# A first pair of projections by eight half products, its operand sums beside it, in a float32 decoder layer

## The chip, the core and the metric

The kernel runs on one core of one Trainium2 chip. The metric is the device time of one execution in microseconds (us). The engines are TensorE (PE; its weight loads are the rows PEld), VectorE (DVE), ScalarE (ACT), GpSimd (POOL) and SyncE (SP), which issues most DMAs. Each runs its own list of instructions in order, and they meet at semaphores: an instruction that waits holds back everything behind it on its engine.

## The reference, cut to what matters

One decoder layer on 1024 tokens of width 1024, all in float32: an input projection feeds a dilated window attention of 12 heads (three groups of four) and a gated DeltaNet of 8 heads; both are gated and merged, and a SwiGLU follows.

```
u = rmsnorm(h, norm_mix[layer])
proj = u @ w_in[layer]
qa, ka, va, qd, kd, vd, z, beta_raw, a_raw, gate_raw = jnp.split(proj, split_at, axis=-1)
...
beta = jax.nn.sigmoid(beta_raw)
g = -jnp.exp(a_log[layer]) * jax.nn.softplus(a_raw + dt_bias[layer])
```

The change concerns the first blocks of `u @ w_in` and how `beta` and `g` are made beside them.

## The kernel before, in words

Activations are held transposed (feature on the partition, 1024 tokens along the row). A float32 matrix product is made of three passes (PASSES): each operand is split into a rounded high part (ACT copies it, L985 for weights) and a low part (POOL or DVE subtracts, L946, L446), and high x high, high x low, low x high are added in a PSUM bank. One matmul has a 128x128 weight block and 512 tokens.

The attention stage makes 24 pairs of 128-column blocks of `w_in`, numbered q = 0 to 23. For unit n = q // 2 (one head; slot s, group g), the even pair gives its queries and keys, the odd pair its values and a block of the gates. A pair by the plain method takes eight half products of 12 matmuls (two blocks, two halves of the tokens, two halves of the 1024 features). The kernel uses Strassen's scheme in Winograd's form and takes seven: PRODUCTS lists them in the order m = 0 to 6 by their weight operand, a, c, s2, s1, s3, s4, d. Weight halves a, c come from `raw_first`, b, d from `raw_second`; s1 = b + d, s2 = s1 - a, s3 = a - b, s4 = c - s2 are made by POOL. The activation operands t1 to t4 are sums of quarters of u (`own_sum_t`), made once by DVE (L488), cast by ACT (operand_cast, L441) and subtracted by DVE (operand_low, L446). They are used by all 24 pairs, as are x11, x21, x22, parts of u itself. t2 is then written over the one quarter of u that is not needed (a copy is kept in DRAM).

The order of the work is written out by hand. Each product has four steps j, so a unit has 56 (j = 0 to 55). At a product's last step ACT takes products 0, 2, 3 and 6 out of PSUM (take_act, L1066), DVE adds 1, 4 and 5 (L1088). Two banks are used in turn, so product m = 2 can start only when product 0 has been taken, m = 4 only when 2 has been taken, and so on (the waits at L1011). Behind these steps ACT casts the next pair's weight operands as HIGH_STEP says, POOL makes that pair's sums and low parts (attention_pool), and SP loads the weights of the pair after it into the same two buffers when the low parts that read them are there (load_first, load_second). Between the matmuls of unit n the softmax steps of unit n - 1 run (att_pe, att_act, at the steps AT: 15 steps for two of the groups, 9 for the third), and at slots 1 to 3 also the mixing of the three groups of the slot before (MIX, with small DMAs that ACT issues at L867 to L873).

Ahead of this stands the set-up: rows of x are scaled (DVE, L457), transposed (PE, L513), weighted (DVE, L472) and split (ACT L417, POOL L356). `beta_decay` (L500) makes the 16 columns for beta and decay in 48 matmuls, 24 of them between the last transposes. The rows of beta and decay are worked out in 40x1024 tiles during unit 0 (decay_act, decay_vec): beta is 1/(1 + exp(-x)), with a reciprocal on DVE (L607).

Of the kernel before, what the change touches and what calls it, by code (L numbers as in the profile page):

```python
# [65 lines left out]
def build(nc, x, norm_mix, w_in, conv_w, a_log, dt_bias, dn_norm, w_proj_attn, w_proj_delta,  # L66
          w_out, norm_ffn, w_gate, w_up, w_down, norm_final, out):
    ctx = ExitStack()
    with ctx:
# [364 lines left out]
        OPERAND = {"t1": 1, "t2": 2, "t3": 3, "t4": 4}  # L434

        def operand_cast(act, o):

# [4 lines left out]

        def operand_low(dve, o):
# [3 lines left out]
                                    ALU.subtract).then_inc(qp["low"], 1)  # L447

        def setup_vec(dve):
# [29 lines left out]
            def part(k_half, t_half):  # L479
                return u32[:, 4 * t_half:4 * t_half + 4, 4 * k_half:4 * k_half + 4, :]  # L480

            def by_chunk(o):
                return own_sum[o][:, :, :].rearrange("p f (c t) -> p c f t", t=P)

            for o, first, second in (("t1", part(0, 1), part(0, 0)), ("t2", part(1, 1), by_chunk("t1")),
                                     ("t3", part(1, 1), part(0, 1)), ("t4", part(1, 0), by_chunk("t2"))):
# [5 lines left out]
            operand_low(dve, "t2")  # L492

        def setup_pe(pe):
# [12 lines left out]
            for c in range(KT):  # L507
# [8 lines left out]
                if c >= KT // 2:  # L516

                    if c == KT // 2:
                        pe.wait_ge(ba_split, 1)
                        pe.wait_ge(x_low, KT)  # L520
                    for k in (2 * c - KT, 2 * c - KT + 1):
                        beta_decay(0, k)
            pe.wait_ge(x_low, 2 * KT)
            for k in range(KT):
                beta_decay(1, k)
# [2028 lines left out]
```

## Time and profile before

| | us |
|---|---|
| median of 3 runs (2327.79 to 2329.65) | 2329.26 |
| profiled execution, its own time | 2330.01 |
| its span in the trace | 2328.3 |
| PE busy | 2205.2 (95% of the span) |
| DVE busy | 1079.8 (46%) |
| ACT busy | 937.3 (40%) |
| POOL busy | 694.2 (30%) |

In 40 slices of 58 us PE is at nine tenths or more in all but the first, one at about 1610 us, one near it and the last; in the first slice it is at five tenths. The granted TensorE clock has a mean of 0.98 of full speed over the span.

A row of the timeline has the start in us, the duration in us, engine, line, operation, tile written <- tiles read, sizes, a count where several are put together, and in brackets how long the engine was idle before it and what ended that. The duration of a matmul in such a row overlaps the next one; from start to start they are 0.227 us apart at full clock, 0.427 at half.

### The profile page before, as it was taken

The numbers are of one execution on the slowest core, as the hardware profiler recorded it, in microseconds if no ns is written. First come the engines' busy times: TensorE is split into PE (matmuls) and PEld (weight loads), VectorE is DVE, ScalarE is ACT, GpSimd is POOL, SyncE is SP. The second block draws the span as 40 slices with busy tenths as digits, with TensorE's granted clock in tenths as the row PEclk, the third lists the DMA queues.
The fourth block names the chain that finished last, engine by engine and source line by source line (L and its number), as shares of the span: only waits on it lengthen the run. The fifth ranks groups of instructions, "written<-read, shape, count | busy, mean of one in ns | idle before, by whom it ended". The sixth has DMA issues, their size and how long they took to land.

```text
span 2328.3 us, 30636 instructions
## 1 busy us (share of the span) xinstructions
PE 2205.2 (95%) x11016; PEld 1829.3 (79%) x11016; DVE 1079.8 (46%) x1470; ACT 937.3 (40%) x1597; POOL 694.2 (30%) x536
## 2 busy tenths in 40 slices
PE   5599999999999999999999999997899999999997
PEld 4488788787887888888888887885688888878886
DVE  6622331323237666656656543423755555550153
ACT  5344444444435545555654641122433333330012
POOL 6487565656522111111111124321000000043330
PEclk8799999999999999999999999998899999999999
DMA  5122212222132202211221343331122222261221
GB/s 111 29 60 68 74 55 65 87 69 74 55 94 80 64 18 72 63 36 45 63 61 29 127 150 114 93 87 45 55 82 81 81 81 81 81 223 48 89 56 73
DMA packets 249953, 175.64 MB, mean 75 GB/s; under 512 B 41272, under 2 KB 225784, under 8 KB 249872
## 3 DMA queue, kind: packets, MB, share of 16 engines
q1 hardware_dynamic: 219808, 136.46, 20.0%
q10 hardware_dynamic: 30064, 38.10, 5.2%
q8 instruction: 51, 0.84, 0.1%
q14 instruction: 30, 0.25, 0.0%
HBM read 143.36 MB, written 31.18 MB: 75 GB/s over the span
## 4 chain that ended last, share of the span: by engine, by line
PE 87%; DVE 5%; ACT 2%; issue 2%; DMA 1%; DVEq 1%; ACTq 1%; POOL 0%; SPq 0%; POOLq 0%
PE bank L213 20%; PE bank L2070 18%; PE bank L1013 16%; PE bank L2298 10%; PE bank L1218 5%; PE bank L1468 2%; PE bank L1451 2%; PE bank L701 1%; PE bank L1458 1%; DVE own_sum_t L488 1%; PE bank L712 1%; PE bank L1505 1%; PE bank L1500 1%; PE bank L1501 1%; PE bank L1487 1%
## 5 line engine op out<-in xcount | busy, mean ns | idle before, releaser
L213 PE MATMUL bank<-u_hi,w_hi 128*128 128x512 f32 x704 | 311.5, 442 | 6.1 <-ACT z_next L1685 4.8
L199 POOL CAST w_hi<-raw 128x1024 fp32r<-128x1024 f32 (+1 forms) x60 | 62.0, 1034 | 726.4 <-PE bank L213 511.6
L213 PE MATMUL bank<-u_hi,w_lo 128*128 128x512 f32 x704 | 277.0, 393 | 0.0
L213 PE MATMUL bank<-u_lo,w_hi 128*128 128x512 f32 x704 | 276.4, 393 | 0.0
L2258 POOL CAST dn_hi<-dn_raw 128x896 fp32r<-128x896 f32 (+1 forms) x24 | 26.0, 1085 | 590.6 <-DMA dn_raw<-in_w_down 482.3
L213 PEld LDWEIGHTS bank<-u_hi,w_lo 128*128 128x128 f32 x704 | 132.5, 188 | 29.3
L201 POOL TENSOR_TENSOR w_lo<-raw,w_hi 128x1024 fp32r<-128x1024 f32 (+1 forms) x60 | 149.0, 2483 | 8.6
L213 PEld LDWEIGHTS bank<-u_hi,w_hi 128*128 128x128 f32 x704 | 134.0, 190 | 22.2 <-ACT z_next L1685 5.3
L946 POOL TENSOR_TENSOR q_lo_s<-q_sum_s,q_hi_s 128x512 fp32r<-128x512 f32 x96 | 125.5, 1312 | 79.9 <-ACT q_hi_s L985 74.2
L213 PEld LDWEIGHTS bank<-u_lo,w_hi 128*128 128x128 f32 x704 | 134.2, 191 | 14.9 <-issue 1.9
L2298 PE MATMUL bank<-v_hi,dn_lo 128*128 128x512 f32 x352 | 136.9, 389 | 0.0
L2298 PE MATMUL bank<-v_lo,dn_hi 128*128 128x512 f32 x352 | 136.9, 389 | 0.0
L2298 PE MATMUL bank<-v_hi,dn_hi 128*128 128x512 f32 x352 | 136.9, 389 | 0.0
L1013 PE MATMUL bank<-u_hi,q_hi_s 128*128 128x512 f32 x192 | 85.0, 443 | 24.6 <-DVE u_lo L446 12.1
L1753 DVE SCALAR_TENSOR_TENSOR conv_out<-conv_in,conv_c,conv_out 128x1024 f32<-128x1024 f32 (+1 forms) x96 | 100.6, 1048 | 14.9 <-issue 12.0
L2070 PE MATMUL bank<-t_hi_t,p_hi_s 128*128 128x512 f32 x264 | 103.2, 391 | 2.7 <-ACT gate_out L2093 2.7
L2070 PE MATMUL bank<-t_hi_t,p_lo_s 128*128 128x512 f32 x264 | 103.4, 392 | 0.0
L2070 PE MATMUL bank<-t_lo_t,p_hi_s 128*128 128x512 f32 x264 | 103.3, 391 | 0.0
L1631 DVE COPY_PREDICATED inv<-merge_mask,bank 128x256 f32<-128x256 uint8 x96 | 45.7, 492 | 105.7 <-PE bank L1468 105.4
L985 ACT ACTIVATE q_hi_s<-q_sum_s 128x512 fp32r<-128x512 f32 x96 | 59.9, 629 | 79.6 <-POOL q_sum_s L961 27.4
L1013 PE MATMUL bank<-own_hi_t,q_hi_s 128*128 128x512 f32 x192 | 78.5, 409 | 7.2 <-ACT qa L1066 6.6
L2097 ACT ACTIVATE gate_out<-gate_out 128x512 f32<-128x512 f32 x44 | 27.8, 632 | 142.5 <-DVE gate_out L2113 142.5
(367 smaller groups left out, 5605.2 us busy)
## 6 DMA issues: line engine op xcount, KB each, us to landing
raw<-in_w_in SPq DMA_DIRECT2D x36, 512.0 KB, 3.9
raw_first<-in_w_in SPq DMA_DIRECT2D x24, 512.0 KB, 3.9
raw_second<-in_w_in SPq DMA_DIRECT2D x24, 512.0 KB, 4.6
row<-scr_rows ACTq DMA_DIRECT2D x24, 512.0 KB, 4.7
raw_gate<-in_w_gate SPq DMA_DIRECT2D x22, 512.0 KB, 4.0
raw_up<-in_w_up SPq DMA_DIRECT2D x22, 512.0 KB, 3.9
scr_v<-gate_out SPq DMA_DIRECT2D x44, 256.0 KB, 2.6
v_in<-scr_v SPq DMA_DIRECT2D x11, 1024.0 KB, 8.5
```

The source lines that it names most:

```text
L199: nc.gpsimd.tensor_copy(hi[:, 0:kt, :], raw[slot][:, 0:kt, :])
L201: nc.gpsimd.tensor_tensor(lo[:, 0:kt, :], raw[slot][:, 0:kt, :], hi[:, 0:kt, :].bitcast(F32), ALU.subtract).then_inc(weights_split, 1)
L213: last = nc.tensor.matmul(bank[dst][:, :], wpart[slot][wp][:, k, :], rhs[ap][:, k, half * HALF:(half + 1) * HALF], start=k == 0 and (wp, a ...
L946: g.tensor_tensor(q_lo[name][:, :, :], src, q_hi[name][:, :, :].bitcast(F32), ALU.subtract).then_inc(qp["part"], 1)
L985: nc.scalar.activation(q_hi[name][:, :, :], src, ACT.Copy).then_inc(qp["high"], 1)
L1013: last = nc.tensor.matmul(bank[D0 + (m + q) % 2][:, :], (q_hi, q_lo)[wp][name][:, kk, :], (ops_hi, ops_lo)[ap][o][:, kk, :], start=m in (0 ...
L1218: last = nc.tensor.matmul(bank[dst][:, :], wpart[slot][wp][:, k, :], (b_hi, b_lo)[ap][t][:, half * HALF:(half + 1) * HALF], start=start an ...
L1451: last = mm(by_block(chunk(bank[Y0], q), level), chunk(a_right, q), side_columns(inv[:, 2 * q * P:2 * (q + 1) * P], level, 0), start=True, ...
L1468: last = mm(bank[Z0 + half][:, (q % 2) * P:(q % 2 + 1) * P], chunk(inv_t, q), half_pair[:, q, :], start=True, stop=True)
L1753: last = v.scalar_tensor_tensor(conv_out[:, part], shifted, tap, conv_out[:, part], ALU.mult, ALU.add)
L2070: last = nc.tensor.matmul(dst[:, :], (p_hi, p_lo)[wp][name][:, kk, :], (t_hi, t_lo)[ap][o][:, kk, :], start=i in (0, 1, 3) and kk == 0 and ...
L2298: last = nc.tensor.matmul(bank[DN_BANKS[g % 2][i][half]][:, :], dn_part[(n + i) % 4][wp][:, k, :], (v_hi, v_lo)[ap][(k0 + k) // 2][:, (k0 ...
```

## The change

- Pair 0 is made by the plain method: eight half products (96 matmuls instead of 84) from u itself (first_pair_pe), in four outputs FIRST_OUT of 24 matmuls each, which ACT takes (first_pair_act). The first unit has 60 steps instead of 56, 32 of them for pair 0. Pair 0 needs no sums, of weights or of u; pair 1 is the first that does.
- The order in which operands are made: t1 (DVE) and t3 (now POOL, third_sum_pool, behind pair 0's low parts), then t2 and t4. ACT casts t1 and t3 before pair 0, t2 and t4 at steps 32 and 34, behind pair 0; t2 has to wait until pair 0 has read the quarter of u that it overwrites.
- All 48 matmuls of beta_decay stand behind the last transpose.
- beta is made as exp(-ln(1 + exp(-x))) on ACT: an addition and the reciprocal leave DVE, an Ln and an Exp on 8 rows come to ACT. The steps of the decay rows are moved back by some steps.
- For all pairs from 1 on POOL's order and ACT's table change: s4 is made before s3, and ACT casts s3 behind s4 at the last product's step instead of one product earlier; the next load of `raw_first` waits for s3's low part, which is now the later of the two.

```diff
-            part_high(act, 0, "a")
-            part_high(act, 0, "c")
+            for name in ("a", "c", "b", "d"):
+                part_high(act, 0, name)
             operand_cast(act, "t1")
-            part_high(act, 0, "s1")
-            part_high(act, 0, "s2")
-            act.wait_ge(ba_done, 2)
-            operand_cast(act, "t2")
-            for name in ("s3", "s4", "d"):
-                part_high(act, 0, name)
+            operand_cast(act, "t3")
...
+            if o == "t2":
+                act.wait_ge(qp["done"], 7)
+            elif o == "t4":
+                act.wait_ge(qp["low"], 3)
...
+        def third_sum_pool(pool):
+            for c in range(4):
+                last = nc.gpsimd.tensor_tensor(by_chunk("t3")[:, c], u_part(1, 1)[:, c], u_part(0, 1)[:, c], ALU.subtract)
+            last.then_inc(ba_split, 1)
...
             operand_low(dve, "t1")
-            operand_low(dve, "t2")
...
-                f(row_t[1][a8, :], row_t[1][a8, :], ACT.Ln, bias=1.0).then_inc(ba_act, 1)
+                f(row_t[1][a8, :], row_t[1][a8, :], ACT.Ln, bias=1.0)
+                f(row_t[1][b8, :], row_t[1][b8, :], ACT.Ln, bias=1.0)
+                act.drain()
+                f(rows[a8, :], row_t[1][b8, :], ACT.Exp, scale=-1.0).then_inc(ba_act, 1)
...
-            v.tensor_scalar(row_t[1][b8, :], row_t[1][b8, :], 1.0, None, ALU.add)
...
-            v.reciprocal(rows[a8, :], row_t[1][b8, :])
...
-        PART_AT = {"a": 1, "c": 2, "s1": 3, "s3": 4, "s2": 5, "s4": 6, "d": 7}
+        PART_AT = {"a": 1, "c": 2, "s1": 3, "s2": 4, "s4": 5, "s3": 6, "d": 7}
...
-                sp.wait_ge(qp["part"], 7 * (q - 1) + PART_AT["s4"])
+                sp.wait_ge(qp["part"], FIRST_PART_AT["c"] if q == 1 else 7 * (q - 1) + PART_AT["s3"])
...
-        HIGH_STEP = {1: ("a",), 2: ("c",), 4: ("s1", "s2"), 5: ("s3",), 6: ("s4",)}
+        HIGH_STEP = {1: ("a",), 2: ("c",), 4: ("s1", "s2"), 6: ("s4", "s3")}
...
+        def first_pair_pe(pe, j):
+            o, k = j // 8, j % 8
+            low_part, high_part, half = FIRST_OUT[o]
+            name = low_part if k < 4 else high_part
+            if k % 4 == 0:
+                pe.wait_ge(qp["part"], FIRST_PART_AT[name])
+                if k == 0:
+                    wait(pe, qp["copied"], o - 1)
...
+            if q == 1 and m == 0:
+                pe.wait_ge(qp["copied"], 3)
```

ACT's list ahead of pair 1's third product, behind the cast for pair 0: before, s1, s2 and s3 (q_hi_s_136, 135, 137) were cast between the takes of pair 0 (L1066), with the decay's Exp and Ln (L543 to L546) between.

```order
L543 ACTIVATE row_t_159<-row_t_158 8x1024
L544 ACTIVATE row_t_159<-row_t_160 8x1024
L546 ACT_TABLE_LOAD
L546 ACTIVATE row_t_159<-row_t_159 8x1024
L1066 ACTIVATE ka_175<-bank 128x512
L985 ACTIVATE q_hi_s_136<-q_sum_s_150 128x512
L985 ACTIVATE q_hi_s_135<-q_sum_s_149 128x512
L985 ACTIVATE q_hi_s_137<-q_sum_s_151 128x512
L1066 ACTIVATE ka_175<-bank 128x512
```

The same place now (q_hi_s_138 is s4, q_hi_s_137 is s3; the L441 rows cast t2 and t4; L1046 takes pair 0, L1125 pair 1):

```order
L546 ACTIVATE row_t_159<-row_t_159 8x1024
L547 ACTIVATE row_t_159<-row_t_159 8x1024
L549 ACT_TABLE_LOAD
L549 ACTIVATE rows<-row_t_159 8x1024
L1046 ACTIVATE ka_175<-bank 128x512
L1004 ACTIVATE q_hi_s_136<-q_sum_s_150 128x512
L1004 ACTIVATE q_hi_s_135<-q_sum_s_149 128x512
L1046 ACTIVATE ka_175<-bank 128x512
L1004 ACTIVATE q_hi_s_138<-q_sum_s_152 128x512
L1004 ACTIVATE q_hi_s_137<-q_sum_s_151 128x512
L441 ACTIVATE u_hi<-own_sum_t_132 128x4x512
L441 ACTIVATE own_hi_t_125<-own_sum_t_131 128x2048
```

The Ln, a table load and the Exp stand in front of the third take, and all casts of sums and of t2 and t4 stand behind it.

ACT's list at the end of an even pair in unit 1, before: the softmax's Exp (L759), the take of product 6, the casts, then the copy of transposed probabilities and the take of the next pair's product 0 (va_t).

```order
L985 ACTIVATE q_hi_s_137<-q_sum_s_151 128x512
L759 ACTIVATE score_181,stat<-score_181,neg_max 128x256 x2
L1066 ACTIVATE ka_177<-bank 128x512
L985 ACTIVATE q_hi_s_138<-q_sum_s_152 128x512
L767 ACTIVATE prob_t_182<-bank 128x512
L1066 ACTIVATE va_t<-bank 128x512
L985 ACTIVATE q_hi_d<-raw_second 128x512
```

The same place now:

```order
L762 ACTIVATE score_181,stat<-score_181,neg_max 128x256 x2
L1125 ACTIVATE ka_177<-bank 128x512
L1004 ACTIVATE q_hi_s_138<-q_sum_s_152 128x512
L1004 ACTIVATE q_hi_s_137<-q_sum_s_151 128x512
L770 ACTIVATE prob_t_182<-bank 128x512
L1125 ACTIVATE va_t<-bank 128x512
L1004 ACTIVATE q_hi_d<-raw_second 128x512
```

The cast of s3 has moved from ahead of the Exp to between the cast of s4 and the take of va_t.

POOL's list for one pair, before (q_lo_s_143, 144, 142, 145 are the low parts of s1, s3, s2, s4):

```order
L946 TENSOR_TENSOR q_lo_s_143<-q_sum_s_150,q_hi_s_136 128x512
L961 TENSOR_TENSOR q_sum_s_151<-raw_first,raw_second 128x512
L946 TENSOR_TENSOR q_lo_s_144<-q_sum_s_151,q_hi_s_137 128x512
L965 TENSOR_TENSOR q_sum_s_152<-raw_first,q_sum_s_149 128x512
L946 TENSOR_TENSOR q_lo_s_142<-q_sum_s_149,q_hi_s_135 128x512
L946 TENSOR_TENSOR q_lo_s_145<-q_sum_s_152,q_hi_s_138 128x512
L946 TENSOR_TENSOR q_lo_d<-raw_second,q_hi_d 128x512
```

The same now:

```order
L956 TENSOR_TENSOR q_lo_s_143<-q_sum_s_150,q_hi_s_136 128x512
L977 TENSOR_TENSOR q_sum_s_152<-raw_first,q_sum_s_149 128x512
L956 TENSOR_TENSOR q_lo_s_142<-q_sum_s_149,q_hi_s_135 128x512
L956 TENSOR_TENSOR q_lo_s_145<-q_sum_s_152,q_hi_s_138 128x512
L982 TENSOR_TENSOR q_sum_s_151<-raw_first,raw_second 128x512
L956 TENSOR_TENSOR q_lo_s_144<-q_sum_s_151,q_hi_s_137 128x512
L956 TENSOR_TENSOR q_lo_d<-raw_second,q_hi_d 128x512
```

The sum s3 (q_sum_s_151) stands behind the low part of s4 (q_lo_s_145), which needs the cast of s4.

## Rows read from the trace of the kernel before

**Rows 1.** The page: chain that ended last by engine; loads of weights.

```profile
PE 87%; DVE 5%; ACT 2%; issue 2%; DMA 1%; DVEq 1%; ACTq 1%; POOL 0%; SPq 0%; POOLq 0%
...
raw_first<-in_w_in SPq DMA_DIRECT2D x24, 512.0 KB, 3.9
```

**Rows 2.** Timeline of PE, 60 to 130 us: start, duration, idle before.

```profile
70.07 0.77 PE L1013 MATMUL bank<-u_hi,q_hi_s 128*128 128x512 f32 x1 [12.15 <-DVE u_lo L446]
...
87.67 0.77 PE L1013 MATMUL bank<-u_hi,q_hi_s 128*128 128x512 f32 x1 [7.85 <-ACT ka L1066]
...
101.53 0.76 PE L1013 MATMUL bank<-own_hi_t,q_hi_d 128*128 128x512 f32 x1 [8.40 <-DVE ka L1088]
...
127.18 0.39 PE L1013 MATMUL bank<-u_hi,q_hi_a 128*128 128x512 f32 x1
```

**Rows 3.** Timeline of DVE, 34 to 96 us.

```profile
34.60 0.69 DVE L472 TENSOR_TENSOR u<-bank,norm_mix_c 128x512 f32<-128x512 f32 x1 [3.38 <-PE bank L513]
...
40.94 6.37 DVE L488 TENSOR_TENSOR own_sum_t<-u 128x512 f32<-128x512 f32 x4
47.40 6.70 DVE L488 TENSOR_TENSOR own_sum_t<-u,own_sum_t 128x512 f32<-128x512 f32 x4
...
58.80 6.58 DVE L488 TENSOR_TENSOR own_sum_t<-u,own_sum_t 128x512 f32<-128x512 f32 x4
65.48 2.29 DVE L446 TENSOR_TENSOR own_lo_t<-own_sum_t,own_hi_t 128x2048 fp32r<-128x2048 f32 x1
...
75.12 0.91 DVE L589 MEMSET reset<- 8x1024 f32 x1
...
81.13 1.22 DVE L598 TENSOR_TENSOR row_t<-row_t,row_t 8x1024 f32<-8x1024 f32 x1
...
88.92 6.54 DVE L607 RECIPROCAL rows<-row_t 8x1024 f32<-8x1024 f32 x1
```

**Rows 4.** Timeline of POOL, 39 to 47 us.

```profile
39.21 5.87 POOL L356 TENSOR_TENSOR u_lo<-u,u_hi 128x512 fp32r<-128x512 f32 x4 [0.19 <-ACT u_hi L417]
45.04 1.72 POOL L946 TENSOR_TENSOR q_lo_a<-raw_first,q_hi_a 128x512 fp32r<-128x512 f32 x1
```

**Rows 5.** Timeline of ACT, 82 to 92 us.

```profile
84.55 1.28 ACT L546 ACT_TABLE_LOAD   x1
85.85 1.05 ACT L546 ACTIVATE row_t<-row_t 8x1024 f32<-8x1024 f32 x1
```

**Rows 6.** Timeline of ACT, ends of pairs 2 and 22.

```profile
155.54 0.62 ACT L985 ACTIVATE q_hi_s<-q_sum_s 128x512 fp32r<-128x512 f32 x1
...
156.54 0.59 ACT L1066 ACTIVATE va_t<-bank 128x512 f32<-128x512 f32 x1
...
638.27 0.61 ACT L985 ACTIVATE q_hi_s<-q_sum_s 128x512 fp32r<-128x512 f32 x1
```

**Rows 7.** Timeline of PE: product 2 of pairs 3 and 23 starts.

```profile
159.63 0.39 PE L1013 MATMUL bank<-u_hi,q_hi_s 128*128 128x512 f32 x1
...
641.34 0.39 PE L1013 MATMUL bank<-u_hi,q_hi_s 128*128 128x512 f32 x1
```

**Rows 8.** Timeline of POOL, 316 to 320 us: the sum s3.

```profile
316.43 1.29 POOL L961 TENSOR_TENSOR q_sum_s<-raw_first,raw_second 128x512 f32<-128x512 f32 x1
```

**Rows 9.** Timeline of ACT, 315 to 327 us: its cast, and the next pair's take.

```profile
317.76 0.63 ACT L985 ACTIVATE q_hi_s<-q_sum_s 128x512 fp32r<-128x512 f32 x1 [2.07 <-POOL q_sum_s L961]
...
323.19 0.60 ACT L1066 ACTIVATE qa<-bank 128x512 f32<-128x512 f32 x1 [1.03 <-PE bank L1013]
```

**Rows 10.** Timeline of ACT, pair 7 (unit 3, mixing of slot 0).

```profile
253.28 0.34 ACTq L867 DMA_DIRECT2D few<-scr_stat  x1
...
259.26 0.63 ACT L985 ACTIVATE q_hi_a<-raw_first 128x512 fp32r<-128x512 f32 x1 [5.82 <-issue]
```

**Rows 11.** Timeline of PE: matmuls behind short waits later in the kernel.

```profile
1417.17 0.47 PE L1218 MATMUL bank<-b_hi,w_hi 128*128 128x512 f32 x1 [2.40 <-DVE b_lo L1209]
...
1418.07 0.63 PE L1218 MATMUL bank<-b_hi,w_hi 128*128 128x512 f32 x1
...
2061.14 0.47 PE L2070 MATMUL bank<-t_hi_t,p_hi_d 128*128 128x512 f32 x1 [1.82 <-DVE up_out L2113]
```

More of the change, by code:

```diff
@@ L477, in setup_vec @@
             dve.wait_ge(consts, 3)
[L479 to L486, printed above, removed]
+            for o, first, second in (("t1", u_part(0, 1), u_part(0, 0)), ("t2", u_part(1, 1), by_chunk("t1")),
+                                     ("t4", u_part(1, 0), by_chunk("t2"))):
                 for c in range(4):
@@ L515, in setup_pe @@
                     last.then_inc(x_turned, 1)
[L516 to L525, printed above, removed]
+            pe.wait_ge(ba_split, 1)
+            for half in range(2):
+                pe.wait_ge(x_low, KT * (half + 1))
+                for k in range(KT):
+                    beta_decay(half, k)
         b8, a8 = slice(0, 8), slice(32, 40)
@@ L959, in attention_pool @@
             low("s1", s1)
-            free("s3")
-            g.tensor_tensor(s3, ra, rb, ALU.subtract).then_inc(qp["sum"], 1)
-            pool.drain()
-            low("s3", s3)
             free("s4")
@@ L997, in restore_vec, with first_pair_act @@
                                     ALU.subtract).then_inc(qp["low"], 1)
+        def first_pair_pe(pe, j):
[6 more added lines that the diff above has]
+                    wait(pe, qp["copied"], o - 1)
+            for wp, ap in PASSES:
+                last = nc.tensor.matmul(bank[D1 - half][:, :], (q_hi, q_lo)[wp][name][:, k % 4, :],
+                                        act_in[ap][:, k, half * HALF:(half + 1) * HALF],
+                                        start=k == 0 and (wp, ap) == PASSES[0], stop=k == 7 and (wp, ap) == PASSES[-1])
+            if k == 7:
+                last.then_inc(qp["done"], 1 if o == 3 else 2)
+        def first_pair_act(act, j):
+            if j % 8 != 7:
+                return
+            o = j // 8
+            half = o % 2
+            act.wait_ge(qp["done"], (2, 4, 6, 7)[o])
+            if o == 0:
+                act.wait_ge(qp["sums"], 3)
+                act.wait_ge(ba_split, 2)
+                act.wait_ge(x_low, 2 * KT)
+            nc.scalar.activation(qk_t[0][o // 2][:, half * HALF:(half + 1) * HALF], bank[D1 - half][:, :], ACT.Copy,
+                                 scale=1.0 if o // 2 else float(P) ** -0.5).then_inc(qp["copied"], 1)
+            if o == 1:
+                part_high(act, 1, "a")
+                part_high(act, 1, "c")
+            elif o == 2:
+                part_high(act, 1, "s1")
+                part_high(act, 1, "s2")
+            elif o == 3:
+                part_high(act, 1, "s4")
+                part_high(act, 1, "s3")
         def dense_att_pe(pe, s, g, j):
@@ L1057, in take_act @@
             act.wait_ge(qp["done"], 7 * q + m + 1)
-            if q == 0 and m == 0:
-                act.wait_ge(qp["sums"], 4)
             if p == 1 and m == 0:
@@ L1102, in attention @@
                     steps = att_steps((g + 2) % 3) if s or g else []
-                    for j in range(56):
-                        dense(eng, s, g, j)
-                        if s == 0 and g == 0:
+                    first = s == 0 and g == 0
+                    for j in range(60 if first else 56):
+                        if not first:
+                            dense(eng, s, g, j)
+                        elif j < 32:
+                            dense_first(eng, j)
+                        else:
+                            dense(eng, s, g, j - 4)
+                        if first:
                             extra(eng, j)
```

115 lines of the change are left out of this document (73 added, 42 removed).

## The prediction

> **What bounds the kernel now.** I read the page's chain of waits first: PE holds 87% of it [rows 1], so time is gained where PE idles and lost where anything makes it wait. Then I read PE's timeline from the start until it no longer idles. It waits three times in pair 0: 12.15 us before the third product until DVE has made t2's low part, 7.85 us before the sixth until ACT takes a half of ka, and 8.40 us before the seventh until DVE adds to ka [rows 2]. The first is the end of four sums and two low parts on DVE; the other two stand behind the decay's work on ACT and DVE, the reciprocal of 6.54 us among it [rows 3]. From 101.53 us PE runs on; pair 2 starts at 127.18 us [rows 2]. These two stretches are what the change is at; the third thing I read is what its new order does to pairs 1 to 23, where PE has hardly any slack.
>
> I use the start of pair 2 as the mark: the start's gain is how much earlier it comes, and all later costs are counted from there.
>
> **The start.** Removed: the beta products between the transposes. DVE waited 3.38 us for a transpose behind them [rows 3], and a further 0.5 us of such waits at the last one goes too; u is complete about 3.9 us earlier, at 37.0 instead of 40.9 us.
> Three sums remain on DVE, t1, t2, t4: 6.37 + 6.70 + 6.58 us [rows 3] with 0.3 us between, so they end at 57.0. These durations hold with POOL at work beside them, as it will be.
> The third sum goes to POOL. It ends its low parts of u at about 42.6, four low parts of weights at 1.72 us [rows 4] take it to 49.5, and the sum is four instructions. The trace has none of that form; the nearest rows are 1.47 (5.87 for four) and 1.72 us [rows 4], so 5.9 to 6.9 us, and it ends between 55.4 and 56.4. I take 56.2. ACT's cast of it is over at 58.1. DVE wants it at 59.3, behind t1's low part of 2.29 us [rows 3]: hidden, with 1.2 us to spare.
> Low t1 and low t3 end at 61.5. From the end of the last such low part (74.98) to the end of the decay's first block it was 7.37 us (81.13 + 1.22 = 82.35) [rows 3], so this block ends at 68.9. ACT has copied the beta rows by 60.
> Now the new path on ACT: two Exp (2.1 us), the table load with its gap (1.3), an Ln of 1.05 [rows 5], as before 4.5 us; new are a second Ln (1.05), a second table load (1.3) and an Exp (1.05), 3.4 us. The forms on 8 rows are those of the rows, so I take them as they stand; the bounds are 3.2 and 3.8. They end at 76.9.
> On this point the Trainium skill ("ScalarE: Activation LUTs", What ACT_TABLE_LOAD costs) says that each switch costs about 1.28 us for the load and 1.38 more for a drain. The first part agrees with the trace, the second doesn't: Ln starts 1.30 us after the load does [rows 5]. By the page the new switch would be 1.4 us dearer and the result 1.4 us later.
> PE meanwhile: beta products until 49, pair 0 in 96 matmuls of 0.227 us, 21.8 us, to about 71. They are 12 more than before (2.7 us), but PE waits behind them in any case: pair 1 needs the bank of the third output, whose take stands on ACT behind the Exp. So PE starts pair 1 at 77.5 and ends its second product at 82 to 85. It then needs t2, and the take of its product 0.
> ACT from 76.9 on [order of ACT above]: take 0.5, casts of s1 and s2 1.15, take 0.5 (79.1). Then it goes to and fro with POOL: low s1, sum s4, ACT's cast of s4 (starts at 80.9), low s2, low s4, sum s3 at 1.25 to 1.3 us each, ACT's cast of s3 (from 84.8), cast of t2 1.9 (87.2), DVE's low t2 2.3 (89.5), ACT's cast of t4 1.9, and only then the take of product 0 (92.0). Product 2 starts at 92.2.
> Behind a wait of 7 us or more TensorE ran at its lower level: the burst behind 7.85 us had a mean granted clock of 0.5, the one from 101.53 needed 5.2 us for 12 matmuls, the one from 70.07 4.2 [rows 2]. So product 2 ends at 96.4 to 97.4. The other four with the eight transposes took 12.0 us up to 127.18 before. Pair 2 starts at 109.4 (108.4 to 109.4 by this alone). The gain of the start is 17.8 us. Its bounds: no contention on DVE's sums at their end and the quick burst, 21; half a us more at each of the eight hand-overs, 14.
>
> **All pairs after it.** Here the change has a price that its start hides. The cast of s3 has moved behind the cast of s4, but POOL makes the sum s3 only behind the low part of s4, which waits for that cast. ACT stands still for a round trip at each pair's end: from the start of the cast of s4 until POOL starts 0.69 us, low s4 1.25, sum s3 1.29 [rows 8], 0.04 to ACT (316.43 + 1.29 = 317.72, cast at 317.76 [rows 9]). The cast of s3 starts 3.26 us after the cast of s4. Queued behind it on ACT are the copy of probabilities and the take of the next pair's product 0, and PE's product 2 waits for that take.
> *Even to odd pair, units with 15 side steps, eight places.* Cast of s4 at 155.54, take of va_t at 156.54 + 0.59, product 2 at 159.63 [rows 6, 7]: 2.5 us of slack, against 3.26 + 0.52 (one more cast, pipelined) = 3.8 us that the take moves. By start times: 155.54 + 3.26 + 0.52 + 0.48 + 0.59 + 0.14 = 160.53, PE loses 0.9. At the last, 638.27 + 4.99 = 643.26 against 641.34: 1.9. The eight are 0.9, 1.9, 1.6, 1.9, 1.1, 1.9, 1.5, 1.9, together 12.8 us.
> *Even to odd, units 3, 6, 9.* The six small DMAs of the mixing are issued by ACT from 253.28, and the next instruction is at 259.26 [rows 10]; they start 2.0 us later, the takes behind them set PE already, so 2.0 each: 6.0 us.
> *Odd to even, eleven places.* The take of product 0 was at 323.19 with product 2 at 326.62; it comes at 321.52 + 3.78 = 325.30 and is done at 325.9: in time. The load of raw_first waits for the low part of s3, 3.1 us later, and lands 3.9 us after its issue [rows 1], so ACT's Exp comes about 1 us later, where there is about 1 us of slack. I take 0.1 for eight of these and 0.5 for the three beside the mixing: 2.3 us.
> Together 21.1 us, bounds 17 and 27: the upper end if a third of the stops also bring the lower clock. A stop of 2.40 us did (0.63 us matmuls from 1418.07, eight of them, 1.6 us lost), one of 1.82 us did not [rows 11]; mine are up to 1.9.
>
> **The sum.** 2328.3 - 17.8 + 21.1 = 2331.6 us of span; the execution's own time lies 1.7 us over its span, which gives 2333.3, and that execution was 0.75 us above the median shown. Forecast against the median: 2329.26 + 3.3 = 2332.6 us. What a measurement can tell from no change is 0.2%, 4.7 us, so this is "within", next to "slower".
>
> **Rivals.**
> *The round trip is hidden (faster).* If ACT's order left it slack, because the stops at product 2 swallow waits that come anyway (1.6 us at product 5 in the mixing units, up to 1.5 at product 4), only the start counts: 2329.26 - 17.8 = 2311.5, or about 2320 if half is swallowed. Against it: eight of the places have no such wait behind them. 13%.
> *The clock falls at the stops (slower).* One mechanism: a stop of 1.9 us at product 2, 11 times, each followed by eight matmuls at the lower level, 1.6 us. It decides if a stop under 2 us is enough. 17.6 us more: 2350. For it: 2.40 us was enough; against it: 1.82 was not [rows 11]. 6%.
> *The start gives less (slower).* The path through ACT at the start has eight hand-overs and a form that the trace lacks (the sum on POOL, strided over u). If POOL's sum runs at 2.5 us an instruction, the cast of t3 comes at 61 and everything behind it 3 to 4 us later: 2336 to 2338. 12%.
> *The change doesn't shorten what it says:* pair 0 now ends early, but PE waits before pair 1 and in it (6 + 8 us). That is in my sum; it is why 28 us of waits give 18.
>
> **Chances.** Forecast case 69%, its own range 2328 to 2337: 2% of it faster, 40 within, 27 slower. Hidden: 13%, of it 11 faster, 2 within. Clock 6% and weaker start 12%: slower, 2 of it within. Faster 0.13, within 0.44, slower 0.43. The range of 8 in 10 is 2321 to 2340: it leaves out the full hidden case and the full clock case.
>
> **What would show it.** In the changed profile: PE waits of 5 to 8 us before pair 1's first product (released by ACT's take of ka) and before its third (released by the take of va_t); pair 2's first matmul at 109 us. From pair 2 on, a wait of 1 to 2 us before product 2 of odd pairs, put down to ACT va_t, in place of none; ACT's cast q_hi_s waiting about 2.7 us for POOL's q_sum_s (L982) some 22 times, 60 us in all. The end of the attention stage about 3 us later than before. Wrong would be: no waits at product 2 of odd pairs, or lower clock behind them, or pair 2's start outside 106 to 113.

## The result and the profile after

The changed kernel takes 2344.1 us (median of 4, 2342.29 to 2348.8) against 2328.59 us beside it: ratio 1.0068, interval 1.0052 to 1.0084. It is slower, and outside the forecast range (2332.6, 2321 to 2340). The sign of each half was right: the start gains, the pairs after it lose. The start gave 14.7 us instead of 17.8, inside its bounds (14 to 21); the pairs took 28.8 instead of 21.1, beyond theirs (17 to 27).

The page's chain of the changed kernel: PE holds 73% of it instead of 87% [rows 1]; POOL, its queue and "issue" have come in.

```profile
PE 73%; issue 6%; POOL 6%; DVE 4%; POOLq 4%; ACT 3%; DMA 2%; ACTq 1%; DVEq 1%; SPq 0%
```

PE's timeline, to set beside [rows 2]:

```profile
77.42 0.76 PE L1074 MATMUL bank<-u_hi,q_hi_a 128*128 128x512 f32 x1 [6.95 <-ACT ka L1046]
...
95.36 0.77 PE L1074 MATMUL bank<-u_hi,q_hi_s 128*128 128x512 f32 x1 [10.90 <-ACT va_t L1125]
...
112.51 0.39 PE L1074 MATMUL bank<-u_hi,q_hi_a 128*128 128x512 f32 x1
```

Two waits of the three are left, now in pair 1, and pair 2 starts at 112.51 instead of 127.18. Up to the second wait the forecast held to 0.3 us: the sums ended at 57.0, the decay's first block at 68.6 (forecast 68.9), ACT's new path at 76.7 (76.9), pair 1 started at 77.4 (77.5), s4's cast at 80.9 (80.9). Then it broke: s3's cast came at 88.0 instead of 84.8, and product 2 of pair 1 (its third, as they count from 0) at 95.36 instead of 92.2. POOL's timeline from 77 us on shows the piece:

```profile
77.87 1.28 POOL L956 TENSOR_TENSOR q_lo_s<-q_sum_s,q_hi_s 128x512 fp32r<-128x512 f32 x1 [10.33 <-ACT q_hi_s L1004]
79.11 1.73 POOL L977 TENSOR_TENSOR q_sum_s<-raw_first,q_sum_s 128x512 f32<-128x512 f32 x1
81.00 4.74 POOL L956 TENSOR_TENSOR q_lo_s<-q_sum_s,q_hi_s 128x512 fp32r<-128x512 f32 x2 [0.16 <-issue]
85.71 2.24 POOL L982 TENSOR_TENSOR q_sum_s<-raw_first,raw_second 128x512 f32<-128x512 f32 x1
```

and DVE's beside it:

```profile
79.79 3.19 DVE L615 TENSOR_TENSOR_SCAN rows<-reset,row_t 8x1024 f32<-8x1024 f32 x1
83.00 1.62 DVE L616 TENSOR_SCALAR row_t<-rows 8x1024 f32<-8x1024 f32 x1
84.69 2.12 DVE L619 TENSOR_TENSOR row_t<-rows 8x1024 f32<-8x1024 f32 x1
```

In the kernel before, the first two of these stood beside an idle POOL:

```profile
96.52 2.28 DVE L612 TENSOR_TENSOR_SCAN rows<-reset,row_t 8x1024 f32<-8x1024 f32 x1
98.81 0.68 DVE L613 TENSOR_SCALAR row_t<-rows 8x1024 f32<-8x1024 f32 x1
```

The same POOL operations took 1.25 to 1.3 us in the rows that the forecast used [rows 8]; here they take 1.73, 4.74 for two, and 2.24 us, 3.6 us more in all. DVE's scan takes 3.19 us instead of 2.28, and the operation behind it 1.62 instead of 0.68. The two engines slow each other; e4 below tests it.

From pair 2 on the loss sits where s3 moved. ACT at the end of pair 22, and PE's product 2 of pair 23, to set beside [rows 6, 7]:

```profile
650.40 0.62 ACT L1004 ACTIVATE q_hi_s<-q_sum_s 128x512 fp32r<-128x512 f32 x1
653.67 0.63 ACT L1004 ACTIVATE q_hi_s<-q_sum_s 128x512 fp32r<-128x512 f32 x1 [2.65 <-POOL q_sum_s L982]
...
654.68 0.59 ACT L1125 ACTIVATE va_t<-bank 128x512 f32<-128x512 f32 x1
```

```profile
655.41 0.47 PE L1074 MATMUL bank<-u_hi,q_hi_s 128*128 128x512 f32 x1 [1.21 <-ACT va_t L1125]
```

The casts are 3.27 us apart (forecast 3.26); over the whole kernel ACT waits 64.6 us for the sum s3, once 6.5 us in pair 1 and 22 times 2.6 us, 58.1 in all, in the pairs' casts (forecast 60):

```profile
L1004 ACT ACTIVATE q_hi_s<-q_sum_s 128x512 fp32r<-128x512 f32 x92 | 57.5, 630 | 119.6 <-POOL q_sum_s L982 64.6 <-POOL q_sum_s L970 20.4 <-POOL q_sum_s L973 10.4
```

The loss of a pair is how much longer it takes, from its first matmul to that of the next pair, than in the kernel before. The first column is the forecast; the other kernels are those of the next section, e2 the kernel before with the new order alone, e1 and e3 the changed kernel with the order undone and with the round trip removed:

| us against the kernel before | forecast | changed | e2 | e1 | e3 |
|---|---|---|---|---|---|
| pair 2 starts | -17.8 | -14.7 | +2.3 | -15.7 | -19.0 |
| 8 odd pairs beside 15 side steps | 12.8 | 9.9 | 9.7 | -0.1 | -0.3 |
| pairs 7, 13, 19 (mixing) | 6.0 | 9.2 | 8.6 | 0.2 | 1.9 |
| pairs 8, 14, 20 | 1.5 | 8.1 | 4.2 | 1.3 | 1.5 |
| 8 other even pairs | 0.8 | 1.6 | 3.4 | -0.2 | 0.6 |
| sum of pairs 2 to 23 | 21.1 | 28.8 | 25.8 | 1.3 | 3.6 |

Behind the attention stage nothing differs: in the last 1670 us PE is busy for 1614.5 us in the trace before and 1614.7 in the one after.

The mixing pairs are what was most underrated. ACT's small loads in pair 7, to set beside [rows 10], and PE:

```profile
243.07 0.34 ACTq L870 DMA_DIRECT2D few<-scr_stat  x1
...
247.71 2.19 ACTq L876 DMA_DIRECT2D few<-scr_stat  x1
250.00 0.63 ACT L1004 ACTIVATE q_hi_a<-raw_first 128x512 fp32r<-128x512 f32 x1 [6.50 <-issue]
250.54 0.58 ACT L1125 ACTIVATE va_t<-bank 128x512 f32<-128x512 f32 x1
```

```profile
251.26 0.76 PE L1074 MATMUL bank<-own_hi_t,q_hi_s 128*128 128x512 f32 x1 [2.43 <-ACT va_t L1125]
251.82 0.63 PE L1074 MATMUL bank<-own_lo_t,q_hi_s 128*128 128x512 f32 x1
...
265.04 0.47 PE L1074 MATMUL bank<-u_hi,q_hi_c 128*128 128x512 f32 x1 [0.76 <-ACT gate_part L1125]
...
269.87 0.47 PE L1074 MATMUL bank<-u_hi,q_hi_s 128*128 128x512 f32 x1 [0.94 <-ACT qa L1125]
...
279.31 0.47 PE L1074 MATMUL bank<-own_hi_t,q_hi_s 128*128 128x512 f32 x1 [1.95 <-ACT qa L1125]
```

The six issues start 1.5 us later in the pair than before and take 6.83 us instead of 5.87. Product 4 waits 2.43 us for the take behind them, and the matmuls after it are 0.63 us long, the lower clock. This clock adds nothing here: PE is 2.44 us late at the start of product 4 and 2.42 at that of product 5, where a wait of 1.60 us has gone. In pair 8, PE waits at product 1 (for the take of gate_part), at product 2 (the take behind the round trip) and 1.95 us at product 4 (before: 0.94 us), since a's cast and the Exps behind it come later.

### The profile page after: what moved, and what is told of

Its sections match the earlier page's. It is cut to its first block, busy times and chain, and to the rows that moved or that the text cites. A ratio compares the mean times of both kernels' runs of the same rounds, so it can differ in the third digit from the quotient of the medians.

```text
span 2342.4 us, 30639 instructions
## 1 busy us (share of the span) xinstructions
PE 2214.5 (95%) x11028; PEld 1833.6 (78%) x11028; DVE 1064.3 (45%) x1461; ACT 932.4 (40%) x1596; POOL 689.5 (29%) x533
## 4 chain that ended last, share of the span: by engine, by line
PE 73%; issue 6%; POOL 6%; DVE 4%; POOLq 4%; ACT 3%; DMA 2%; ACTq 1%; DVEq 1%; SPq 0%
PE bank L213 19%; PE bank L2135 17%; PE bank L2363 10%; PE bank L1074 6%; PE bank L1283 5%; POOL q_lo_s L956 2%; PE bank L1533 2%; PE bank L1516 2%; DMA raw_first<-in_w_in 1%; POOLq L983 1%; POOLq L978 1%; POOL q_sum_s L982 1%; PE bank L1523 1%; POOLq L971 1%; POOLq L974 1%
## 5 line engine op out<-in xcount | busy, mean ns | idle before, releaser
L956 POOL TENSOR_TENSOR q_lo_s<-q_sum_s,q_hi_s 128x512 fp32r<-128x512 f32 x92 | 120.4, 1310 | 108.4 <-ACT q_hi_s L1004 102.4
L1004 ACT ACTIVATE q_hi_s<-q_sum_s 128x512 fp32r<-128x512 f32 x92 | 57.5, 630 | 119.6 <-POOL q_sum_s L982 64.6
L1074 PE MATMUL bank<-own_hi_t,q_hi_s 128*128 128x512 f32 x184 | 77.4, 421 | 19.2 <-ACT qa L1125 10.3
```

The costliest lines, as they stand in the source:

```text
L956: g.tensor_tensor(q_lo[name][:, :, :], src, q_hi[name][:, :, :].bitcast(F32), ALU.subtract).then_inc(qp["part"], 1 if q or name != "d" else 4)
L1004: nc.scalar.activation(q_hi[name][:, :, :], src, ACT.Copy).then_inc(qp["high"], 4 if q == 0 and name == "d" else 1)
L1074: last = nc.tensor.matmul(bank[D0 + (m + q) % 2][:, :], (q_hi, q_lo)[wp][name][:, kk, :], (ops_hi, ops_lo)[ap][o][:, kk, :], start=m in (0 ...
```

## The experiments

Times are medians with the ratio to the kernel before on the same chip; where no interval stands there was one execution.

**e1: only the order of s3 and s4 undone.**

```diff
-        PART_AT = {"a": 1, "c": 2, "s1": 3, "s2": 4, "s4": 5, "s3": 6, "d": 7}
+        PART_AT = {"a": 1, "c": 2, "s1": 3, "s3": 4, "s2": 5, "s4": 6, "d": 7}
-        HIGH_STEP = {1: ("a",), 2: ("c",), 4: ("s1", "s2"), 6: ("s4", "s3")}
+        HIGH_STEP = {1: ("a",), 2: ("c",), 4: ("s1", "s2"), 5: ("s3",), 6: ("s4",)}
```

POOL's block for s3 and the wait of raw_first's load go back with it.

> The changed kernel with one part undone: s3 is again made before s4 and cast one product earlier, for all pairs from 1 on, and the load of raw_first waits for s4's low part again. The changed kernel's trace loses 28.8 us between pair 2's start and the last product of pair 23 against the kernel before. Theory A, all of these 28.8 us come from the new order (each stop begins at ACT's standing still between the casts of s4 and s3): they go, pair 2 starts within 1 us of 112.5, the time is 2344.1 - 28.8 = 2315, ratio to before 0.994. Theory B, the order costs the 21.1 us of the prediction and the rest comes from something else in the change (the later mixing DMAs, the decay rows): 2323, ratio 0.9975. Theory C, the order is swallowed by other waits and the loss is elsewhere: above 2330.

Measured 2315.32 us, ratio 0.9948 (0.9935 to 0.9962). Theory A holds for all but a little: of the 28.8 us in pairs 2 to 23, 27.5 are gone, and pair 2 starts 1.1 us earlier. The 1.3 us that stay are in pairs 8, 14 and 20. There PE still waits at product 1 for the take of gate_part, and starts it 0.6 to 1.0 us late, with the order undone and the mixing on time:

```profile
258.22 0.47 PE L1074 MATMUL bank<-u_hi,q_hi_c 128*128 128x512 f32 x1 [0.66 <-ACT gate_part L1125]
```

In the changed kernel it starts 0.7 to 1.2 us late, in e2 0.2, 0.0 and 0.0. So this piece comes with another part of the change, not with the order. On ACT the gate's store stands behind a small load of mixed rows, issued 1.8 to 2.5 us behind the store that it waits for; before and in e2 it was 1.4, and 1.4 to 1.5 in e6, e9 and e10, which have t3's sum on DVE. e6 undoes that sum alone, and PE's waits at product 1 are 0.34, 0.00 and 0.52 us there instead of 0.76, 1.09 and 1.19. This points at the sum on POOL, by one trace; how it would act so late stays open.

**e2: the kernel before with only the new order** (the diff above, reversed).

> The kernel before with this one part of the change: s4 before s3 on POOL and ACT, s3 cast behind s4 at the last product's step, raw_first's load behind s3's low part; pair 0 still by seven products. Theory A (all 28.8 us of the steady loss are the order's): 2328.6 + 28.8 = 2357, ratio 1.012, and pair by pair the same steps as in the changed kernel: 0.9 or 1.4 us at product 2 of odd pairs, 2 to 4 us at product 4 of pairs 7, 13, 19, about 2.6 us in pairs 8, 14, 20. Theory B (21.1 us): 2350, ratio 1.009. Theory C: within 0.2% of before.

Measured 2357.7 us, ratio 1.0135 (1.0119 to 1.0151). The time is that of theory A (2357), in part by luck: the pairs lose 25.8 us in the trace, not 28.8, and 2.3 more are lost ahead of pair 2. The steps in the table are at the same products, but smaller behind the mixing (4.2 against 8.1 us) and larger in the other even pairs. Nothing of the plain first pair is needed to make most of the loss.

**e3: the round trip taken away, the casts left where they are.**

```diff
             free("s4")
+            free("s3")
             g.tensor_tensor(s4, rc, s2, ALU.subtract).then_inc(qp["sum"], 1)
+            g.tensor_tensor(s3, ra, rb, ALU.subtract).then_inc(qp["sum"], 1)
             pool.drain()
             low("s2", s2)
             low("s4", s4)
-            free("s3")
-            g.tensor_tensor(s3, ra, rb, ALU.subtract).then_inc(qp["sum"], 1)
-            pool.drain()
             low("s3", s3)
```

> The changed kernel, order of casts as it is (s4, then s3, both at the last product's step), but POOL makes the sum s3 directly behind the sum s4, before the low parts of s2 and s4. ACT then finds s3 ready when it has cast s4: the round trip is gone, one cast more stays in front of the take. Theory A (the round trip is the cost): casts 0.5 us apart, no stop at product 2 of odd pairs (0.5 us against 2.5 us of slack), nearly all of the 28.8 us gone, 2315 to 2318. Rival: the moved cast and the later load of raw_first are the cost, the gap between the casts is harmless: 2335 or more, with the stops where they are.

Measured 2315.59 us, ratio 0.995 (0.9936 to 0.9963). ACT's casts at the end of pair 22 are now one group of two, 1.14 us in all, and the stop at pair 23's product 2 is gone:

```profile
622.33 1.14 ACT L1003 ACTIVATE q_hi_s<-q_sum_s 128x512 fp32r<-128x512 f32 x2
...
623.85 0.59 ACT L1124 ACTIVATE va_t<-bank 128x512 f32<-128x512 f32 x1
```

So nearly all of the cost is that POOL made s3 behind a low part that waits for ACT. It was paid in pair 1 too: pair 2 starts 4.3 us earlier here. Of the 3.6 us that the pairs still lose, 1.3 are in e1 as well. The other 2.3 belong to the later cast and the later load, which this run does not separate; most of them are beside the mixing, where the six issues take 6.0 to 6.3 us (e1: 5.4 to 5.6).

**e4: POOL left alone by the scan in pair 1.** The scan and what follows it stand behind pair 1's first add; the transposes of the decay rows go into pair 2 (their edit isn't shown).

```diff
-            elif j == 42:
+            elif j == 40:
+                decay_scan(dve)
+            elif j == 52:
                 decay_third(dve)
```

> The changed kernel, with the decay's scan and the two operations behind it moved on DVE from step 20 to step 40 of the first unit (behind t4's low part), and what follows them (ACT's Exps, stores, the eight transposes) moved back too, the transposes into pair 2. In the changed kernel POOL needs 1.73, 3.08, 1.71 and 2.24 us for four instructions of 1.28 us that lie beside these DVE operations, 3.6 us more. Theory: the two engines slow each other; with DVE idle there POOL's four take 1.3 us each from the scan's place on (the first, beside the short ones that stay, may keep 0.4 of it), the cast of s3 starts 3.2 us earlier (84.8 instead of 88.0) and pair 1's third product at 92.2 instead of 95.4; the time is about 3 us less. Rival: POOL is slow there for a reason of its own (these tiles, DMA traffic): the durations stay, the third product stays at 95.4.

The mechanism came out to 0.1 us. POOL and PE:

```profile
80.91 2.54 POOL L961 TENSOR_TENSOR q_lo_s<-q_sum_s,q_hi_s 128x512 fp32r<-128x512 f32 x2 [0.16 <-issue]
83.40 1.29 POOL L987 TENSOR_TENSOR q_sum_s<-raw_first,raw_second 128x512 f32<-128x512 f32 x1
```

```profile
92.11 0.77 PE L1079 MATMUL bank<-u_hi,q_hi_s 128*128 128x512 f32 x1 [7.66 <-ACT va_t L1130]
...
114.34 0.64 PE L573 MATMUL bank<-ident,rows 128*128 128x128 f32 x2 [3.59 <-ACT per_token L563]
```

Two low parts take 2.54 us instead of 4.74, product 2 of pair 1 starts at 92.11 (95.36 in the changed kernel). The time did not fall, 2344.86 in the one execution: the moved transposes now stopped PE for 3.59 us, and pair 2 lost 6.3 us where 3.2 had been won at product 2. The expected 3 us at the end was wrong.

**e5: the reciprocal back on DVE.**

```diff
-                f(row_t[1][a8, :], row_t[1][a8, :], ACT.Ln, bias=1.0)
-                f(row_t[1][b8, :], row_t[1][b8, :], ACT.Ln, bias=1.0)
-                act.drain()
-                f(rows[a8, :], row_t[1][b8, :], ACT.Exp, scale=-1.0).then_inc(ba_act, 1)
+                f(row_t[1][a8, :], row_t[1][a8, :], ACT.Ln, bias=1.0).then_inc(ba_act, 1)
```

> The changed kernel with one part undone: beta's 1/(1 + exp(-x)) by an addition and the reciprocal on DVE, ACT without the second Ln, the second table load and the Exp. Theory A (what starts last in pair 1 is ACT's list, and DVE has room beside it): ACT's third take comes 3.4 us earlier (73.3 instead of 76.7), POOL's chain too and it lies beside the reciprocal, which slowed no POOL operation in the kernel before; the scan then ends about 0.3 us later than now, at 87; t2's low part 87 to 89.3; the third product of pair 1 starts at 91.9 instead of 95.4, the time is 3 us less than the changed kernel's. Theory B (the reciprocal's 6.5 us on DVE hold back t2's low part, as they held back the seventh product in the kernel before): 3.8 us more than the changed kernel's.

2340.97 us; the third product and pair 2 come 2.8 us earlier than in the changed kernel. Theory A: in this place two activations and a table load on ACT (3.5 us) cost more than 6.5 us on DVE.

```profile
73.93 0.76 PE L1073 MATMUL bank<-u_hi,q_hi_a 128*128 128x512 f32 x1 [3.35 <-ACT ka L1045]
...
92.57 0.77 PE L1073 MATMUL bank<-u_hi,q_hi_s 128*128 128x512 f32 x1 [11.37 <-ACT va_t L1124]
```

**e6: t3's sum back on DVE.**

```diff
             for o, first, second in (("t1", ...), ("t2", ...),
+                                     ("t3", u_part(1, 1), u_part(0, 1)), ("t4", ...)):
...
-                if q == 0:
-                    third_sum_pool(pool)
```

> The changed kernel with one part undone: the sum t3 again on DVE, third of four, nothing of it on POOL. Theory: DVE's sums end 6.6 us later (63.7 instead of 57.0), and everything behind them with them: low parts, the decay's first block, ACT's Exp; the third product of pair 1 at 102, the time 6.6 us more than the changed kernel's. Rival: the sums on DVE lost time beside POOL's, so that fewer than 6 us come back: 3 us more or less.

Neither number came: pair 2 starts 0.9 us *earlier* than in the changed kernel, and the one execution took 2343.12 us. The rival's reason holds. DVE's sums:

```profile
43.46 6.71 DVE L491 TENSOR_TENSOR own_sum_t<-u,own_sum_t 128x512 f32<-128x512 f32 x4
50.26 2.50 DVE L491 TENSOR_TENSOR own_sum_t<-u 128x512 f32<-128x512 f32 x4
52.84 2.50 DVE L491 TENSOR_TENSOR own_sum_t<-u,own_sum_t 128x512 f32<-128x512 f32 x4
```

The second sum, beside POOL's low parts, takes 6.71 us for four instructions; the third and fourth, from the moment that POOL has nothing left (49.6 us), 2.50 us each. So the 6.6 us that this sum was expected to cost on DVE is the price beside a busy POOL. The kernel before showed less as well: there t3's four instructions took 4.52 us, from 54.19.

**e8: beta products between the transposes again.**

```diff
+                if c >= KT // 2:
+                    for k in (2 * c - KT, 2 * c - KT + 1):
+                        beta_decay(0, k)
```

> The changed kernel with one part undone: 24 of the 48 beta products stand again between the last transposes. Theory: u is complete 3.9 us later (40.9 instead of 37.0 us), all sums and what follows them too, and the third product of pair 1 comes at 99.3 instead of 95.4; 3.9 us more. Rival: PE's pair 0 ends in time anyway and the sums' delay is taken up by POOL's and ACT's waits: less than 1 us.

Pair 2 starts 3.1 us later than in the changed kernel, near the expected 3.9 (the sums on DVE got 1.2 us shorter). The one time, 2343.74 us, doesn't show it: the last product of pair 23 is still 2.2 us late in the trace, and single executions differ by as much.

**e11: what makes the mixing's issues slow.** e1 with the two loads of a pair issued together:

```diff
-                sp.wait_ge(qp["part"], ... 7 * (q - 1) + PART_AT["s4"])
+                sp.wait_ge(qp["part"], ... 7 * (q - 1) + PART_AT["s4" if q < 3 else "d"])
```

> The changed kernel in the old order s3 before s4 (ACT and POOL as there), with one thing moved: the load of raw_first waits for the low part of d from pair 3 on, so that SP issues the two loads of a pair back to back, some 2.5 us later for raw_first. In the kernel before and in the old order ACT's six issues of the mixing's small loads took 5.4 to 5.9 us in units 3, 6 and 9, in both kernels with the new order 6.8 to 7.2 us; there raw_first's load is issued beside them. Theory A (the issues are slow because the two loads move at the same time): the six take 6.8 us or more here too, ACT's take of product 2 comes 1 to 1.5 us later and PE stops at product 4 of pairs 7, 13 and 19; with the later cast of a behind it about 5 us in all, 2320. Theory B (the issues are slow for what happens on ACT, because they begin later in the pair): they stay at 5.4 to 5.9 us, no stop at product 4, 2315 to 2317.

2320.9 us, ratio 0.9968 (0.9958 to 0.9977): the time of theory A, but not for its reason. The six issues stay at 5.6 us (5.55, 5.67, 5.62); what comes late is the load, for which the cast of a waits behind them:

```profile
241.35 1.61 ACTq L876 DMA_DIRECT2D few<-scr_stat  x1
243.72 0.63 ACT L1004 ACTIVATE q_hi_a<-raw_first 128x512 fp32r<-128x512 f32 x1 [5.87 <-DMA raw_first<-in_w_in]
```

So A falls. In the changed kernel and e2 the two loads are issued 0.6 and 1.9 us behind the first of the six (in pair 19 of the changed kernel 0.4 us ahead of it and 0.9 behind), here 1.4 to 1.8 and 1.8 to 2.2 behind, in e1 1.2 to 1.4 ahead and 1.3 to 1.8 behind. What lengthens the six by 1.0 to 1.8 us in the changed kernel stays open; in pair 19 of e9, which has the old order, they took 6.41 us.

**e7, e9, e10: versions.** e10 undoes three parts together, by the diffs of e1, e5 and e6:

> The changed kernel with three parts undone together: the old order s3 before s4, the reciprocal on DVE, t3's sum on DVE. What stays of the change is the plain first pair and the beta products behind the transposes. Theory (the parts add): 2315.3 (old order alone) - 3.1 (reciprocal) - 0.7 (third sum) = 2311.5, ratio 0.993. Rival: with the old order the scan on DVE, later with the reciprocal, holds back t2's low part, and nothing is gained over the old order alone: 2315.

2312.73 us, 0.9932 (0.9918 to 0.9945): within 1.3 us of the sum of the parts. e7 keeps the plain first pair and takes the decay off the path to pair 1; of its edits the main ones:

```diff
-                f(row_t[1][b8, :], row_t[1][b8, :], ACT.Ln, bias=1.0)
-                act.drain()
-                f(rows[a8, :], row_t[1][b8, :], ACT.Exp, scale=-1.0).then_inc(ba_act, 1)
-            elif j == 36:
+                f(row_t[1][b8, :], row_t[1][b8, :], ACT.Ln, bias=1.0)
+            elif j == 47:
                 act.wait_ge(ba_vec, 3)
+                act.drain()
+                f(rows[a8, :], row_t[1][b8, :], ACT.Exp, scale=-1.0)
...
             elif o == 3:
+                operand_cast(act, "t2")
                 part_high(act, 1, "s4")
...
+            decay_first(dve)
             operand_low(dve, "t1")
+            operand_low(dve, "t3")
```

> A version that should beat both: the changed kernel's first pair, the old order s3 before s4 for pairs from 2 on, and ACT's and DVE's lists of the first unit rearranged so that nothing of the decay stands ahead of pair 1: the row copies and decay's first block directly behind the sums, the Exps and Lns before the third take, t2's cast right behind pair 0, the scan behind the first add of pair 1, beta's Exp with the other Exps behind the fourth product's take, the transposes of the decay rows in the first steps of pair 2. For pair 1 POOL makes all four sums ahead of the low parts, and raw_first is loaded for pair 2 when the sums are made. Theory: PE runs from 48.5 us nearly without a wait (1 us at pair 1's third product), pair 2 starts at 91 instead of 111.5 (the changed kernel in the old order), less 0.9 us for the transposes that lie behind that mark now: 2315.3 - 20 + 1 = 2296, ratio to before 0.986. Rival: POOL and DVE slow each other there and the casts come late, 8 us of it stay: 2304.

2311.0 us, 0.9919 (0.9905 to 0.9933), not 2296. Pair 2 starts at 98.3, but the gain goes in pair 2: against e1 it loses 3.5, 5.4 and 2.1 us up to the starts of its first three products. PE waits 3.45 us for an add behind the decay's last block on DVE, then 2.94 us before a transpose of the decay rows, whose copies out of PSUM stand on ACT behind a cast that waits for POOL, and the matmuls behind these stops run at the lower clock. In the profiled execution 3.7 us more went in pairs 13 and 14, 3.1 of them by the lower clock behind stops of 1.84 and 2.06 us:

```profile
389.29 0.47 PE L1092 MATMUL bank<-u_hi,q_hi_s 128*128 128x512 f32 x1 [1.84 <-ACT gate_part L1143]
...
390.21 0.63 PE L1092 MATMUL bank<-u_hi,q_hi_s 128*128 128x512 f32 x1
```

The five times spread from 2307 to 2313. e9 moves what stood in the way, and puts t3's sum back on DVE (its edit against e7, the main ones):

```diff
-            decay_first(dve)
             operand_low(dve, "t1")
             operand_low(dve, "t3")
+            decay_first(dve)
...
-            elif j == 16:
+            elif j == 24:
                 act.wait_ge(ba_vec, 1)
...
-            elif j == 52:
+            elif j == 55:
                 decay_third(dve)
...
-        TURN_AT = (60, 62, 64, 66)
+        TURN_AT = (72, 74, 76, 78)
```

> The version with the decay beside pair 1, mended at the places where its trace lost time again: t3's sum is back on DVE (beside an idle POOL a sum took 2.50 us there, beside a busy one 6.4 to 6.7), the low parts of t1 and t3 come before the decay's first block and before POOL starts on pair 1, ACT takes the third output before the Exps, the decay's last DVE block stands behind pair 1's last add, the transposes of the decay rows use other banks at steps 12 to 18 of unit 1, and POOL's two small masks are made later. Theory: no PE wait before pair 1, 1 us at its third product, pair 2 starts at 91 to 92 (with the changed kernel in the old order: 111.5) and nothing is given back in pair 2: 2315.3 - 19 = 2296, ratio to before 0.9865. Rival: DVE and POOL still slow each other in pair 1 and pair 2 waits for POOL as it did (some 8 us): 2304.

2302.94 us, 0.9892 (0.9877 to 0.9907), the best of all. PE's waits from 55 us on:

```profile
74.37 0.47 PE L1088 MATMUL bank<-u_hi,q_hi_c 128*128 128x512 f32 x1 [0.98 <-ACT ka L1059]
...
78.71 0.47 PE L1088 MATMUL bank<-u_hi,q_hi_s 128*128 128x512 f32 x1 [1.37 <-DVE u_lo L453]
```

Pair 2 starts at 92.4, near the expected 91 to 92; but 7.7 us are given back in it again, 3.9 of them at product 1, whose bank waits behind POOL's chain. The rival had that, and its 2304. POOL runs late there; its longest low part lies beside DVE's subtraction and t4's low part:

```profile
82.96 4.48 POOL L964 TENSOR_TENSOR q_lo_d<-raw_second,q_hi_d 128x512 fp32r<-128x512 f32 x1
```

## Why the prediction was wrong

The forecast span was 2331.6 us, the measured one 2342.4. Of these 10.8 us, 3.1 are in the start and 7.7 in the pairs, where the terms beside the mixing are 9.8 us short, the other even pairs 0.8 us short, and the eight odd pairs 2.9 us too dear.

**"low s2, low s4, sum s3 at 1.25 to 1.3 us each"** is the step that failed in the start. The durations came from rows late in the stage, and were put beside DVE's scan and its followers. e4 moved these away and got the forecast's 92.2 back (92.11). The 3.1 us missing from the start's gain are all of this term. The durations of the sums held; they came from rows with both engines at work.

**"units 3, 6, 9 ... 2.0 each: 6.0"** and **"0.5 for the three beside the mixing"** are the steps that failed in the pairs: 9.2 and 8.1 us were measured, 9.8 us more than the 7.5 of the forecast. The first took the DMA issues at their old length. They started 1.5, 1.5 and 2.5 us later in the pair, 5.5 in all and near the forecast's 6.0, but they also grew by 1.0, 1.8 and 1.4 us, which the forecast put at nothing. The lower clock behind the stops of 2.43 to 3.50 us added next to nothing: PE was 2.4, 3.0 and 3.7 us late at the start of product 4 and 2.5, 3.2 and 3.5 at the end of the pair. The second counted only the later cast of a. Product 2 pays for the round trip there too (1.11 us in each of the three), product 1 starts 0.7 to 1.2 us late, and 1.9 us more go behind product 2. The piece at product 1 is not the new order's: e1 has 0.6 to 1.0 of it, and ends with 1.3 us in these three pairs. The forecast had no term for it, and its cause is open.

**The eight odd pairs** were overrated, 9.9 against 12.8 (the eight terms as listed add to 12.7): from s4's cast to the take all comes as worked out (650.40 to 654.68, 4.28 us; forecast 4.26), but the cast itself starts sooner relative to PE, 2.78 us behind pair 23's first product where it was 3.43, and this takes up 0.6 of the 1.9 us.

**The mechanism was right**: the gap is 3.27 us, ACT waits 58.1 us at it in 22 pairs, and taking it away (e3) returns 25.2 of the 28.8 us. So was the price of the reciprocal by activations, 3.4 us of ACT (8.0 us of ACT from 68.65 to 76.65, 4.5 before), but the forecast never asked whether it should be compared with the reciprocal's cover on DVE; e5 shows it as a loss of 2.8 us. Nor did the forecast price the third sum against leaving it on DVE; e6 shows that it takes 2.5 us there once POOL is idle, and that moving it lost 0.9 us.

**The rivals.** That the round trip is hidden: no, every one of the eight odd pairs was 0.9 to 1.3 us late at product 2. That the start gives less: yes, 3.1 us, but not by the sum on POOL that it named, whose 6.83 us was in the bounds. That the clock falls at the stops: in the changed kernel not at those of 0.8 to 1.95 us, but at those of 2.43, 2.86 and 3.50 us in the mixing, where it cost next to nothing. The forecast had no case in which two of them came together.

## What to carry to other kernels

When operands pass to and fro between two engines, write down for each operation which side it waits for: a sum that needs nothing from the other engine must not stand behind a low part that does. One sum moved (e3) was worth 28 us of 2344. And a duration is only as good as its neighbour: take it from a row in which the other of DVE and POOL was doing what it will be doing. Of a change in several parts, price each against leaving it out; here three of them lost (the order, the third sum on POOL, the reciprocal on ACT; the last two by one trace each), and the plain first pair did not need the one that lost most (e1).

## What the runs showed of the hardware

DVE and POOL hold each other up in these float32 operations on SBUF. A DVE sum of four instructions takes 2.50 us beside an idle POOL and 6.3 to 6.7 beside a busy one; a POOL low part takes 1.28 us alone, 1.73 beside the sums, and 2.4 to 4.5 beside DVE's scan and low parts. The scan is on 8 partitions and POOL's operands are on 128, and a DVE operation with one tensor input (L616) still went from 0.68 to 1.62 us. Beside DVE's reciprocal of 6.54 us POOL kept its 1.27 us, in the kernel before and in e5. The Trainium skill ("SBUF — State Buffer", SBUF: two separate sides) says that the two engines share a pair of ports which is locked for a whole instruction, also by a DVE operation with two SBUF inputs; if each then waits about one instruction of the other, a DVE instruction of a sum beside POOL takes 0.63 + 1.27 = 1.9 us, an estimate from that rule and this case's durations. The traces agree in direction and roughly in size (1.6 to 1.7).

The length of a stop alone does not tell whether the lower clock follows. In the changed kernel it came behind PE's stops of 2.43, 2.86 and 3.50 us (0.63 us matmuls within 0.6 us) and behind none of up to 1.95 us in pairs 2 to 23. But in e7 it came behind 1.84 and 2.06 us, in e8 behind 2.17, and in e2 and e11 stops of 2.62, 2.75 and 2.76 us were followed by matmuls at full clock, while another of 2.76 us in e11 was not. So [rows 11] are two cases and no bound between them:

```profile
268.21 0.47 PE L1014 MATMUL bank<-own_hi_t,q_hi_s 128*128 128x512 f32 x1 [2.62 <-ACT va_t L1067]
268.51 0.39 PE L1014 MATMUL bank<-own_lo_t,q_hi_s 128*128 128x512 f32 x1
```
